# Last turn of the mixer: the low halves of the eight yr chunks made on GpSimd (Pool) instead of VectorE

## The reference, cut to what matters

```python
y_rnn_x = h_x * jax.nn.gelu(gx)                      # the rnn branch's output
y_na_x = neighborhood_attention(...)                 # the attention branch's output
merged = jax.nn.sigmoid(g_rnn) * (y_rnn @ w_rnn_out) + jax.nn.sigmoid(g_na) * (y_na @ w_na_out)
x = x + mx[2] * (merged @ w_out)
```

## Time and profile before

| | us |
|---|---|
| three runs | 2176.55, 2177.58, 2179.7 |
| median | 2177.58 |
| the profiled execution's own time | 2179.56 |
| its span in the trace | 2177.8 |
| busy over the span: PE | 2087.9 (96%) |
| DVE | 1569.9 (72%) |
| ACT | 1048.8 (48%) |
| POOL | 346.2 (16%) |

### The profile page before, as it was taken

How to read it: one execution, slowest core, us unless ns; L and a number is a source line. 1 busy time by engine, 2 the same in 40 slices (tenths; PEclk the granted TensorE clock), 3 DMA queues, 4 the chain that set the end, 5 groups by cost and what they waited for, 6 DMA issues and landing times.

```text
span 2177.8 us, 28175 instructions
## 1 busy us (share of the span) xinstructions
PE 2087.9 (96%) x10750; PEld 1768.7 (81%) x10750; DVE 1569.9 (72%) x2758; ACT 1048.8 (48%) x1604; POOL 346.2 (16%) x234
## 2 busy tenths in 40 slices
PE   5899999999999999999998899998999999999999
PEld 1778888988888889888896788886888888888887
DVE  6688588585885977859858766667998888873432
ACT  3466666665666656666666520002444334433221
POOL 0031230221212221113022000000111111110000
PEclk9999999999999999999999999998999999999999
DMA  8421212012112120111102474362222212146552
GB/s 321 115 57 40 61 49 64 27 51 68 34 37 68 49 71 29 40 61 49 53 19 97 151 282 174 127 210 81 70 87 88 87 69 77 68 157 209 183 184 89
DMA packets 85654, 209.91 MB, mean 96 GB/s; under 512 B 24592, under 2 KB 30096, under 8 KB 85392
## 3 DMA queue, kind: packets, MB, share of 16 engines
q1 hardware_dynamic: 63360, 182.95, 24.5%
q0 software_dynamic: 5760, 20.97, 2.8%
q10 hardware_dynamic: 16400, 4.19, 0.9%
HBM read 171.39 MB, written 40.89 MB: 97 GB/s over the span
## 4 chain that ended last, share of the span: by engine, by line
PE 80%; DVE 10%; ACT 4%; issue 1%; DMA 1%; POOL 0%; SPq 0%; ACTq 0%; DVEq 0%; POOLq 0%
PE banks L46 14%; PE banks L45 14%; PE banks L47 14%; PE banks L976 4%; PE banks L847 4%; PE banks L849 4%; PE banks L848 4%; PE banks L2073 4%; PE banks L2071 4%; PE banks L2072 4%; PE banks L880 3%; DVE probT_low L1451 2%; PE banks L938 1%; DVE prob L1443 1%; PE banks L920 1%
## 5 line engine op out<-in xcount | busy, mean ns | idle before, releaser
L45 PE MATMUL banks<-qh,xnh 128*128 128x384 f32 (+1 forms) x640 | 223.3, 349 | 0.3 <-PEq L211 0.3
L847 PE MATMUL banks<-xnh,wh 128*128 128x512 f32 (+1 forms) x536 | 211.9, 395 | 2.5 <-ACT stage L1078 2.4
L47 PE MATMUL banks<-qh,xnl 128*128 128x384 f32 (+1 forms) x640 | 207.5, 324 | 0.0
L46 PE MATMUL banks<-ql,xnh 128*128 128x384 f32 (+1 forms) x640 | 207.4, 324 | 0.0
L849 PE MATMUL banks<-xnh,wl 128*128 128x512 f32 (+1 forms) x536 | 204.5, 381 | 0.0
L848 PE MATMUL banks<-xnl,wh 128*128 128x512 f32 (+1 forms) x536 | 204.4, 381 | 0.0
L1451 DVE TENSOR_TENSOR probT_low<-banks,probT_high 128x512 fp32r<-128x512 f32 (+2 forms) x256 | 138.9, 584 | 56.3 <-ACT probT_high L1142 55.3
L46 PE MATMUL banks<-yl,wh 128*128 128x512 f32 x404 | 157.3, 389 | 0.0
L47 PE MATMUL banks<-yh,wl 128*128 128x512 f32 x404 | 157.2, 389 | 0.0
L45 PE MATMUL banks<-yh,wh 128*128 128x512 f32 x404 | 157.2, 389 | 0.0
L1142 ACT CAST probT_high<-banks 128x512 fp32r<-128x512 f32 (+2 forms) x256 | 117.0, 510 | 60.3 <-PE banks L938 52.3
(11 more groups left out here) (344 smaller groups left out, 5828.3 us busy)
## 6 DMA issues: line engine op xcount, KB each, us to landing
raw<-w_ff SPq DMA_DIRECT2D x33, 512.0 KB, 3.7
raw<-w_down SPq DMA_DIRECT2D x33, 512.0 KB, 4.1
raw<-w_fm SPq DMA_DIRECT2D x32, 512.0 KB, 6.6
raw<-w_qkv SPq DMA_DIRECT2D x24, 512.0 KB, 3.9
raw<-w_mix SPq DMA_DIRECT2D x24, 512.0 KB, 5.0
h_d<-conv_d SPq DMA_DIRECT2D x22, 512.0 KB, 2.6
sw_d<-h_d SPq DMA_DIRECT2D x44, 256.0 KB, 2.9
raw<-w_modT SPq DMA_DIRECT2D x16, 512.0 KB, 4.7
```

Of the source, the lines that this page charges most:

```text
L45: pe.matmul(out, w_hi(k), x_hi(k), start=(k == 0), stop=False)
L46: pe.matmul(out, w_hi(k), x_lo(k), start=False, stop=False)
L47: last = pe.matmul(out, w_lo(k), x_hi(k), start=False, stop=(k == chunks - 1))
L847: pe.matmul(out, fh[:, s, k, :], xnh[:, k, c0:c1], start=(k == 0), stop=False)
```

## The change

Pool's function gets `y_low`, with the same waits, operands and count as DVE's had. Pool does the eight subtractions in a row after its last sigmoid of the last turn, each as soon as ACT's rounding copy of that chunk is there. DVE's loop loses them.

```diff
@@ gpsimd(pool) @@
+            def y_low(k):
+                pool.wait_ge(y_in[k % 2], (k // 2 + 1) * 16)
+                pool.wait_ge(y_hi, k + 1)
+                pool.tensor_tensor(yl[:, k, :], raw[:, k % 2, :], yh[:, k, :].bitcast(F32), ALU.subtract)\
+                    .then_inc(y_lo, 1)
...
                     sigmoid(i, LAST_MN + 1, 3, 6)
+                    for k in range(KC):
+                        y_low(k)
@@ vector(dve) @@
-            def y_low(k):
-                dve.wait_ge(y_in[k % 2], (k // 2 + 1) * 16)
-                dve.wait_ge(y_hi, k + 1)
-                dve.tensor_tensor(yl[:, k, :], raw[:, k % 2, :], yh[:, k, :].bitcast(F32), ALU.subtract)\
-                   .then_inc(y_lo, 1)
...
                     if last:
-                        if u % 2 == 1:
-                            y_low(u // 2)
-                        elif u in (2, 6):
+                        if u in (2, 6):
                             mix_low(u // 4)
```

## The result

The changed kernel took 2190.51 us, median of six runs (2188.01 to 2195.94), against 2177.65 (2176.55 to 2179.7) for the kernel before in six: a ratio of 1.0065, with a 95% interval of 1.0055 to 1.0076, or +12.9 us. The forecast was 2184.5 with a range up to 2189.5. Slower was right, and so was the mechanism of the hold. How often the hold came, and what PE's clock did behind it, were not.

The account below looks back on a forecast made before the run. DVE and a ring through the engines were taken to bound the last turn's loop, PE the rest. Relief -1.75, four holds +8.5 and the end +0.2 summed to +6.9 us: 2184.5 us, range 2177.5 to 2189.5.

Parts of the forecast that it names:

- the hold: DVE's minimum L1446, started inside a Pool subtraction, lasts until that ends: 2.1 to 2.2 us lost each, counted in full.
- What bounds: In the last turn's loop DVE, not PE, is the bound; PE runs without a break behind it.
- ring: Last turn's loop, once per two units: PE products and transposes, ACT's cast, DVE's reductions to L1468, PE's next product.
- What L1422 gives, -1.75: Taking eight subtractions off DVE gains 1.05 us at chunk 2 and 0.7 at chunk 0, about nothing elsewhere.
- the first 0.18 us: No profile row showed L1446 starting closer than 0.18 us behind Pool; the forecast took smaller leads as held.
- rival 1: L1446 reads before Pool's first read, so no pair is held: -1.5 us, 2176.1; chance 0.14.
- How many are held, four: L1446 is held behind chunks 1 to 4, where Pool leads by 0.1 to 0.2 us: +8.5 us.
- rival 3: L1446 is held in chunks 5 and 6 too, two more holds of 2.3: +11.5 us, 2189.1; chance 0.09.
- The end, +0.2: PE's piece of chunk 7, after the last product, waits for Pool's last subtraction: +0.2 us.
- The clock at nothing: The sum has no term for PE's clock falling after idle times in the loop.
- a rival with 0.12: PE's clock falls to half after a held pair's idle time: +3 us on top of +6.9, 2187.5; chance 0.12.
- Rivals 3 and 4: In the loop: more minima held, 2189.1, chance 0.09; PE's clock falling as well, 2187.5, chance 0.12.

Follow-up runs that it names:

- memsets: The changed kernel with Pool's eight subtractions replaced by memsets to zero of the same tiles: 2176.08 us, ratio 0.9995.
- filler kernel: The changed kernel with four matmuls of zeros on PE before its wait for a group's output, groups 1 to 6, last turn: 2186.94 us, ratio 1.0046.

## Why the prediction was right and wrong, by its steps

- **What bounds**: right. DVE and its ring set the loop, PE ran on behind it, and the last piece to the end stayed within 0.3 us.
- **What L1422 gives, -1.75**: right in sum. The loop is 2.0 shorter with memsets; with Pool's subtractions and no hold it is 1.8 and 1.9, the end included. Chunks 0 and 2 gave 0.7 and 1.05, as forecast. Two things that it put at nothing nearly cancel: chunk 6's L1422 was on the path too, by 0.4, and DVE's idle 0.26 before chunk 5's minimum puts that 0.35 later.
- **A hold, 2.1 to 2.2 us each, counted in full**: right, with 2.04 to 2.15 for the four of the forecast (leads of 0.07 to 0.17) and 1.95 for the fifth (lead 0.26); each stands in full in the loop. The question left open, the first 0.18 us, is answered: leads of 0.07, 0.09 and 0.17 hold to Pool's end, so rival 1 is out. A minimum that is 0.09 ahead is free.
- **How many are held, four**: this failed. The step was "that both instants hang on the same cast of ACT keeps these distances as the pairs slide". Chunk 5's distance of 0.08 was smaller than a gap of 0.26 that DVE's shifted list put in front of it. It was rival 3 (an L1446 later by that much) for one of its two chunks, and it cost 1.95. The four that were forecast were held with the leads that were forecast.
- **The end, +0.2**: right (PE's weight load waited 0.2 us for Pool's last subtraction; 0.1 in the loop).
- **The clock at nothing**: this failed most. The sum has no term for it. It was a rival with 0.12, and the reason against it, that "most gaps here would be 2.4 to 2.8", took the earlier trace rows's 3.03 as if it were a limit. Gaps of 2.3 to 2.7 were followed by a fall four times in five, and once in the kernel with one chunk moved, while one of 3.31 was not. The price was 1.5 us for a fall of 3.4 us, half of what I gave it, but it came again and again: 7.4 us in the profiled execution. It also made the sixth hold of 1.6.

With the numbers measured, the profiled execution's loop adds up: -2.0 + 10.2 for five holds + 0.1 at the end = +8.3, then 7.4 for the clock and 1.6 for the sixth hold: 17.3 of 17.4. In the medians, the same five holds leave 12.9 - 8.3 = 4.6 for the clock and what it brings; the filler kernel, at +9.4 with its own 0.4 taken off, leaves 3.9. So about 4, with no trace of a median run to split it further. Rivals 3 and 4 were not quite alternatives: chunk 5's hold came without the clock, chunk 6's came from it.

## What to carry to other kernels

Before moving an instruction to Pool, list VectorE's instructions with two SBUF operands that can start within it, even the tiny ones on a critical ring: here 128x1 elements cost 2.1 us each, more than the 1.23 us instruction that was moved off. Start Pool's work behind such an instruction (one wait), or give that one a single operand. Distances of 0.1 us between two engines may not survive a change of the list (one of the five forecast here didn't), so a forecast should count both sides of each; and an idle time on PE is to be priced twice, once as such and once for the clock after it.

## What the hardware showed that I had not expected

- The hold needs hardly any lead: 0.07 us suffice, and 0.09 the other way is free.
- The length of PE's idle time doesn't tell by itself whether its clock falls: behind 2.33 us it fell once and stayed once, behind 3.31 it stayed, all in one loop. What tells them apart no run here shows.
- Not every Pool instruction with SBUF operands holds to its end. The kernel before has a power of 24 columns on Pool, and a subtraction of two SBUF operands that starts 0.04 us behind it takes 1.26 us, against a median of 1.22 for its line. It is so in all seven turns where the two meet. Timeline of the kernel before:

```profile
1120.82 4.17 POOL L798 TENSOR_TENSOR rstd<-rstd,power 128x24 f32<-128x24 f32 x1 [23.57 <-DVE rstd L1357]
1120.86 1.26 DVE L1276 TENSOR_TENSOR wl<-raw,wh 128x1024 fp32r<-128x1024 f32 x1 [0.19 <-ACT wh L1072]
```

Were it held to the end of L798 as L1446 is, it would have taken 4.15. That Pool reads its few columns at the start and computes for the rest would explain it, and wasn't tried.
